# Token-major last products in the second block, and the first mixer's chunks in another order

## The reference

```python
# first block, layer 0: the first mixer (pool_hgrn_mixer), for both streams
z = h @ w_in                                   # u | q | zf | zb | v | g
f = lb + (1 - lb) * sigmoid(zf);  k, logf = 1 - f, log(f)      # and the same for zb
o = hgrn_scan(silu(q), k, v, logf)             # forwards and backwards, decays exp(cumsum(logf))
y = concat([multiscale_pool(u), rmsnorm(o) * silu(g)]) @ w_out
# every layer of the first block: six modulation vectors per layer and stream
m = silu(c) @ ada_w[l] + ada_b[l]
# second block, for each layer i, ALPHA = sqrt(2)
x = layer_norm(ALPHA * x + 0.5 * swiglu(x), g0, b0)
x = layer_norm(ALPHA * x + mixer(x), g1, b1)   # layer 0: window attention + gated recurrence; layer 1: delta rule
x = layer_norm(ALPHA * x + 0.5 * swiglu(x), g2, b2)
x = x + sigmoid(x @ ple_wg + ple_bg) * (p @ ple_wp)
# swiglu(x) = (silu(x @ wg) * (x @ wu)) @ wd, hidden width 2816
```

## Time and profile before

| | |
|---|---|
| median of 3 runs | 2632.01 us (2630.17 to 2641.66) |
| profiled execution | 2630.2 us, span 2628.4 us |
| TensorE busy | 2366.0 us, 90% |
| VectorE, ScalarE, GpSimd busy | 1277.7, 894.1, 120.1 us |
| last chain, share of TensorE | 84% |
| mean granted TensorE clock | 0.945 of full |
| moved from HBM | 370.64 MB, 141 GB/s over the span |

### The profile page before, as it was taken

One profiled execution on the slowest core, in us unless ns is written; L12 is line 12 of the kernel. 1 busy time (PEld: TensorE's weight loads), 2 busy tenths in 40 slices (PEclk: granted clock), 3 DMA queues, 4 the chain that ended last, 5 costly groups with the idle time before them and its releaser, 6 DMA issues.

```text
span 2628.4 us, 39106 instructions
## 1 busy us (share of the span) xinstructions
PE 2366.0 (90%) x17300; PEld 2181.0 (83%) x17300; DVE 1277.7 (49%) x1457; ACT 894.1 (34%) x929; POOL 120.1 (5%) x68
## 2 busy tenths in 40 slices
PE   7988888998899788999799878998899898888997
PEld 5876755998899556999799868998799795878996
DVE  4246425554454243544544545544554586526444
ACT  4212313334333132333433334333333434124332
POOL 0037400000000000000000000000000020000000
PEclk9988998999999999999899989999899996999998
DMA  7246701554355121355355313543354350013451
GB/s 304 98 164 262 289 16 60 180 188 160 133 187 177 71 88 64 144 184 184 128 185 177 129 69 126 188 176 142 130 186 181 108 182 16 1 66 135 177 188 35
DMA packets 52481, 373.10 MB, mean 142 GB/s; under 512 B 5728, under 2 KB 6752, under 8 KB 7840
## 3 DMA queue, kind: packets, MB, share of 16 engines
q1 hardware_dynamic: 51584, 367.78, 38.4%
q0 software_dynamic: 800, 3.93, 0.4%
HBM read 370.64 MB, written 1.05 MB: 141 GB/s over the span
## 4 chain that ended last, share of the span: by engine, by line
PE 84%; DVE 10%; ACT 3%; POOL 1%; issue 1%; DMA 1%; SPq 0%; DVEq 0%; ACTq 0%; POOLq 0%
PE PS L342 10%; PE PS L343 10%; PE PS L344 10%; PE PS L189 7%; PE PS L357 6%; PE PS L356 6%; PE PS L355 6%; PE PS L298 4%; PE PS L645 2%; DVE ring_r L443 2%; PE PS L280 2%; PE PS L263 2%; PE PS L265 2%; PE PS L264 2%; PE PS L281 2%; PE PS L282 2%
## 5 line engine op out<-in xcount | busy, mean ns | idle before, releaser
L443 DVE TENSOR_TENSOR ring_r<-ring,AR_r 128x2048 fp32r<-128x2048 f32 x274 | 625.0, 2289 | 605.8 <-ACT AR_r L437 595.4
L437 ACT ACTIVATE AR_r<-ring 128x2048 fp32r<-128x2048 f32 x274 | 520.1, 1908 | 705.4 <-PE PS L357 306.2
L342 PE MATMUL PS<-AR_r 128*128 128x256 f32 x2240 | 635.3, 284 | 0.0
L343 PE MATMUL PS<-AR_r 128*128 128x256 f32 x2240 | 634.7, 283 | 0.0
L344 PE MATMUL PS<-AR_r,ring_r 128*128 128x256 f32 x2240 | 634.6, 283 | 0.0
L342 PEld LDWEIGHTS PS<-AR_r 128*128 128x128 f32 x2240 | 430.9, 192 | 0.0
L343 PEld LDWEIGHTS PS<-AR_r 128*128 128x128 f32 x2240 | 430.9, 192 | 0.0
L344 PEld LDWEIGHTS PS<-AR_r,ring_r 128*128 128x128 f32 x2240 | 430.9, 192 | 0.0
L355 PE MATMUL PS<-AR_r 128*128 128x256 f32 x1232 | 348.7, 283 | 0.0
L356 PE MATMUL PS<-AR_r 128*128 128x256 f32 x1232 | 348.7, 283 | 0.0
L357 PE MATMUL PS<-AR_r,ring_r 128*128 128x256 f32 x1232 | 348.6, 283 | 0.0
(11 more groups left out here) (346 smaller groups left out, 3290.8 us busy)
## 6 DMA issues: line engine op xcount, KB each, us to landing
ring<-stream SPq DMA_DIRECT2D x346, 1024.0 KB, 4.8
X<-xt SPq DMA_DIRECT2D x1, 2048.0 KB, 10.1
AR<-bias POOLq DMA_DIRECT2D x1, 1536.0 KB, 6.8
AR<-pt POOLq DMA_DIRECT2D x2, 512.0 KB, 3.8
out<-X SPq DMA_DIRECT2D x1, 1024.0 KB, 4.8
SM<-small SPq DMA_DIRECT2D x1, 545.0 KB, 4.1
AR<-invc SPq DMA_DIRECT2D x1, 512.0 KB, 15.3
X<-negl POOLq DMA_DIRECT2D x1, 512.0 KB, 4.0
```

The lines of the kernel that those rows point to most:

```text
L342: pe.matmul(o, w_hi, X_HI[:, k, :], start=(k == 0), stop=False)
L343: pe.matmul(o, w_hi, X_LO[:, k, :], start=False, stop=False)
L437: act.activation(W_HI[i % 3], ring[:, n % SLOTS, :], ACT.Identity).then_inc(split_hi, 1)
L443: dve.tensor_tensor(RING_R[:, n % SLOTS, :], ring[:, n % SLOTS, :], W_HI[i % 3], ALU.subtract).then_inc(split_lo, 1)
```

## The change

Two things change.

In the second block the last products of the six stages come out token-major: token on the partition, feature along the row. The activation is stationary, and 512 columns of weights move past it (`down_tokens`, `pe_out_tokens`). The residual, scaled by 2 ALPHA or ALPHA, is put into the same banks by 16 fp32 matmuls with a scaled identity (`pe_residual_into_tokens`). The LayerNorm then takes its statistics along the row on VectorE (BN_STATS, BN_AGGR), ScalarE makes one column of Ln and Exp, both engines scale half a row each, and TensorE transposes back. The first two chunks of the next stage are split ahead. In the last mixer the logits come behind the first chunks, and the decay rows behind the first convolution.

In the first mixer the chunks come in the order zf, zb, u, q, g, v. Gates, logarithms, running sums and keys (`forget`, `keys_and_sums`), the pooling on GpSimd and the key sum (`KSUM`) have their places between the chunks' splits. The diagonal comes right behind the last chunk, two groups of modulation rows follow instead of six, and the levels hold 18 groups instead of 14. Rows of a batch of up to 12 groups gather in one bank, each at its own offset of the strips `CS`, and are copied and turned together.

```diff
-        EARLY_GROUPS = range(ADA_FIRST, ADA_FIRST + 6)
+        ADA_BATCHES = [range(0, ADA_FIRST), range(ADA_FIRST, 12), range(12, ADA_GROUPS)]
+        EARLY_GROUPS = range(ADA_FIRST, ADA_FIRST + 2)
...
+            def down_tokens(d, i, last, r):
+                n = n0 + i
+                need_split(r, i)
+                for t in range(2):
+                    for h in range(2):
+                        o = PS[:, 2 * t + h, :]
+                        for f in range(2):
+                            w = slice(f * D + h * 512, f * D + (h + 1) * 512)
+                            w_hi, w_lo = W_HI[i % 3][:, w], RING_R[:, n % SLOTS, w]
+                            ts = slice(t * P, (t + 1) * P)
+                            pe.matmul(o, G_HI[:, d, f, ts], w_hi, start=False, stop=False, skip_group_check=True)
+                            pe.matmul(o, G_HI[:, d, f, ts], w_lo, start=False, stop=False, skip_group_check=True)
+                            ins = pe.matmul(o, G_LO[:, d, f, ts], w_hi, start=False, stop=(last and f == 1), skip_group_check=True)
+                        if last and (t, h) != (1, 1):
+                            ins.then_inc(S["tokens_done"], S.mark("tokens_done", (tag, t, h)))
...
+            for t in range(2):
+                act.wait_ge(S["token_stats"], S.at("token_stats", (tag, t)))
+                act.activation(RSTD[:, t:t + 1], MEANVAR[:, t, 1:2], ACT.Ln, bias=EPS[:, eps:eps + 1]).then_inc(order.sem, order.step())
+                act.wait_ge(order.sem, order.n)
+                act.activation(RSTD[:, t:t + 1], RSTD[:, t:t + 1], ACT.Exp, scale=-0.5).then_inc(S["rinv"], S.mark("rinv", (tag, t)))
...
             pool.wait_ge(S["counts_loaded"], S.at("counts_loaded"))
-            pool.wait_ge(S["taken_vector"], S.at("taken_vector", 11))
+            pool.wait_ge(S["taken_vector"], S.at("taken_vector", 5))
...
                 dve_split_chunk(dve, "mix3_in", i + 3)
+                if i == 0:
+                    decay_rows()
```

More of the change, by code:

```diff
@@ L226, in pe_ada_rows @@
+        batch_of = lambda g: next(b for b, gs in enumerate(ADA_BATCHES) if g in gs)
+        ends_batch = lambda g: any(g == gs[-1] for gs in ADA_BATCHES)
         def pe_ada_rows(pe, g):
+            b = batch_of(g)
+            row = 2 * (g - ADA_BATCHES[b][0])
+            if row == 0:
+                pe.matmul(PS[:, b, 0:2], ZERO[:, :], ZERO[:, 0:2], start=True, stop=False, skip_group_check=True)
             for c in range(2):
[L229 removed]
@@ L364, in pe_ffn @@
                 pe.wait_ge(S["residual"], S.at("residual", (earlier, GROUPS - 1)))
-            for b in range(4):
+            for b in range(4) if not token_major else ():
                 pe.matmul(PS[:, b, 0:2], ZERO[:, :], ZERO[:, 0:2], start=True, stop=False, skip_group_check=True)
@@ new lines, in keys_and_sums @@
+            def keys_and_sums(d):
+                dve.wait_ge(S["log_forget"], S.at("log_forget", d))
+                dve.tensor_scalar(K2[:, d, :], K2[:, d, :], -1.0, 1.0, ALU.mult, ALU.add).then_inc(order.sem, order.step())
+                b = B2[:, d, ::-1] if d else B2[:, d, :]
+                for h in range(HEADS):
+                    bh = b[:, h * T2:(h + 1) * T2]
+                    ins = dve.tensor_tensor_scan(bh, RI[:, :], bh, 0.0, ALU.mult, ALU.add)
+                    if h < 3:
+                        ins.then_inc(order.sem, order.step())
+                ins.then_inc(S["log_sums"], S.mark("log_sums", d))
@@ new lines, in pe_out_tokens @@
+        def pe_out_tokens(pe, tag, x):
+            for i in range(4):
+                n = START[tag] + i
+                need_chunk(pe, n)
+                for t in range(2):
+                    for k in range(DT):
+                        ins = pe.matmul(PS[:, 2 * t + i // 2, (i % 2) * 256:(i % 2 + 1) * 256], x[:, k, t * P:(t + 1) * P],
+                                        ring[:, n % SLOTS, k * 256:(k + 1) * 256], start=False, stop=(i % 2 == 1 and k == DT - 1), skip_group_check=True)
+                    if t == 0 and i % 2:
+                        ins.then_inc(S["tokens_done"], S.mark("tokens_done", (tag, t, i // 2)))
+                ins.then_inc(multiplied, 1)
@@ new lines, in pe_layernorm @@
+        def pe_layernorm(pe, tag):
+            for first in (0, 4):
+                for t in range(2):
+                    pe.wait_ge(S["normed"], S.at("normed", (tag, t if first == 0 else 1)))
+                    pe.wait_ge(S["token_high"], S.at("token_high", (tag, t if first == 0 else 1)))
+                    for k in range(first, first + 4):
+                        ins = pe.transpose(turned_at(k)[:, t * P:(t + 1) * P], TOK[:, t, k * P:(k + 1) * P], IDENT)
+                        if t and k % 2:
+                            ins.then_inc(S["turned_back"], S.mark("turned_back", (tag, k // 2)))
```

405 lines of the change are left out of this document (220 added, 185 removed).

## The result

The changed kernel takes 2533.3 us (median of 4 runs, 2532.5 to 2534.4), the kernel before 2635.0 in the same comparison (2630.2 to 2641.7). The ratio is 0.9613, 95% interval 0.9589 to 0.9637; 2520 was forecast, in a range of 2502 to 2544. The profiled execution took 2532.5 us around a span of 2530.8 (before: 2630.2 and 2628.4), so the traces explain 97.6 us of span, and the prediction's sum was 111.2.

What follows compares the result with a forecast made beforehand. TensorE was taken to hold most of the chain, so time is won where it waits or multiplies less. Seven terms sum to 111.2 us off 2630.2, giving 2519, or 2520 against the median; range 2502 to 2544.

Steps and rivals of the forecast that it cites:

- Transfers in the levels: First mixer's levels: 88 us against 98.4, 10.4 us won, allowing 2 for late transfers; the transfers called the doubtful part.
- rival 1: First mixer's levels: transfers bind there, priced at 8 us by the scaled row, giving 2528; chance 0.12.
- The scaled 384: Old level loop's queue rate, 296 GB/s at share 0.77, scaled to a full share; it would give 8 us of waiting.
- The start of the levels: First mixer: the first level product starts at 181.7 instead of 220.1, 38.4 us won.
- rival 3: First mixer: GpSimd and VectorE slow each other more under the projection; 17 us lost, 2537; chance 0.05.
- The down products: Second block: 5.44 us a chunk instead of 5.76, residual +2.8; net 3 us won over four stages.
- rival 4: Down products: wide matmuls with gated activation as weights don't pipeline; slower than before, 2645 and up; chance 0.02.
- The LayerNorm behind a mixer: Second block, two stages: first chunks done at 17.0 against 28.3 us, at full clock; 22.6 us won.
- E+5.3: Behind a mixer: first weight product starts 5.3 us after E, the end of TensorE's last product.
- The LayerNorm behind a feed-forward: Second block, three stages: first product 7.6 us after the last, first chunks taking 12.6; 24.3 us won.
- Rival 2: LayerNorm chain: longer than built, half clock in all six stages; 2.5 us a stage, 15 in all, 2535; chance 0.14.
- ffn4 to the last mixer: Fourth feed-forward stage into last mixer: logits behind first chunks, a 1.9 us stall at chunk 4; 8.9 us won.

Runs made afterwards that it cites:

- half_rows: Changed kernel with only half of each transfer loaded for the 40 chunks of modulation rows behind the projection, matmuls as many as before; 2532.1 us.
- best: Changed kernel with LayerNorm statistics ahead of scaling, last modulation-row copy behind the exponentials, 20 identity transposes in one wait behind a feed-forward stage; 2516.5 us.
- warm_tr: Changed kernel with 16 and 18 identity transposes on TensorE in its LayerNorm waits behind each of the four feed-forward stages; 2519.6 us.
- logits_first: Changed kernel with the last mixer's logits back ahead of its first two chunks and the decay rows ahead of the first convolution; 2532.1 us.
- before_warm: Kernel before with 88 identity transposes on TensorE in its 12 us wait ahead of the first level product; 2629.6 us, ratio 0.9960.
- rows_late: Changed kernel with ScalarE's last modulation-row copy behind the exponentials and first key decay, and VectorE taking the modulation behind the scaled queries; 2532.1 us.

## Why the prediction was right, and where it was short

The forecast was right, and not because errors cancelled: all seven terms came out smaller than I took them, by 0.5 to 5.3 us.

**Transfers in the levels (rival 1).** The doubtful part held. The queue moves nearly what the first row promised (427 GB/s for 12 us) for 50 us on end; two windows of the changed kernel:

```profile
225.00:245.00 20.00, 20.00 (x242) 16.26 (x241) 20.00 (x20) 5.74 (x3) 16.52 (x7) 1.00 1.01 422
245.00:275.00 30.00, 28.00 (x353) 21.04 (x352) 21.87 (x27) 5.74 (x3) 16.88 (x7) 1.00 1.01 419
```

The scaled 384 was no limit. Nor was the 358 that the Trainium skill (DMA: Bandwidth & Descriptors, Where 436 GB/s comes from) gives for reads from HBM, as half of what two cores share: this kernel, on one core, gets 419 to 422. I allowed 2 us for late transfers; half_rows measures 2.6. TensorE's own work is as costed: 14 products spaced 3.71, 18 groups (1.87, 1.80 in pairs) and one turn make 86.0 where I had 86.2. The term is 2.4 short because I left out that VectorE's products hold TensorE for 1.4 us in steps 3 and 4, and the transfers cost 0.6 over the allowance; 0.4 are spread.

**The start of the levels** is 3.3 short. 1.6 of it is the projection, which starts later (65.03 for 63.40). The four first groups are now turned together behind ScalarE's copy; in the chain the last chunk of rows takes 1.98 there, half clock, and the copy 0.61 before the turn. I had costed the batched turn in the levels only. The other 1.6 is one link: I took 2.4 for VectorE's two products and they take 3.9, as they did before (2.74 and 1.15). Reorder and cover (rival 3) were right: the projection takes 110.09 as before, the diagonal follows the last chunk at once, and pooling ends at 151.4 and the key sum (L866) at 153.8, where I had 150 and 154:

```profile
150.08 1.29 POOL L967 TENSOR_TENSOR AR<-AR 128x512 f32<-128x512 f32 x1
...
151.48 2.29 DVE L866 TENSOR_TENSOR AR<-AR 128x2048 f32<-128x2048 f32 x1 [5.27 <-POOL AR L967]
```

**The down products** are spaced 5.47 a chunk (5.44 predicted), so rival 4 is out.

**The LayerNorm behind a mixer** was predicted at E+5.3 and full clock; it is 5.8 and full clock, the first chunks taking 11.7 (here the last product ends at 1537.56):

```profile
1543.39 0.36 PE L289 MATMUL PS<-AR_r 128*128 128x256 f32 x1 [1.59 <-DVE AR_r L494]
```

In `best`, though, one of the two began at half clock (13.9).

**The LayerNorm behind a feed-forward** is the step that was mis-sized, and 5.3 of the missing 13.8. "After a feed-forward I take 12.6": the first chunks take 13.6 to 14.2. BN_STATS is as assumed (0.65). The chain is 0.8 longer, mostly since twelve transposes run at half clock and four gain operations, not two, precede the first split. I had the mechanism, a clock that falls in the wait, but let the last transposes bring it back; warm_tr shows that this takes transposes before the fall. Rival 2 is thus a third true: the chain is 0.8 longer per stage, not 2.5.

**ffn4 to the last mixer**: 8.0 for 8.9, the stall at chunk 4 1.3 for 1.9. By logits_first at most 1.4 of it is the logits' move; the rest is the LayerNorm, which my sum did not separate.

**What the profile did not tell**: the medians differ by 101.7, the profiles by 97.6. The profiled execution of before was its fastest, and in the traces at hand the old levels are where its executions part.

## What to carry to other kernels

A wait that TensorE spends idle can be paid twice, in the wait and at half clock behind it, so an order that shortened it by 1.9 us of 8.4 won nearly twice that; where it can't be shortened, transposes of a constant hold the clock, if they stand ahead of the wait that ends last and fit in it. In a chain of small operations over two halves, do both halves' statistics before either's scaling. And compare stretches between landmarks, not totals, when executions differ by more than the edit.

## What the runs showed of the hardware that was not expected

- Transposes hold the clock as fp32 matmuls do: 1.00 in both fills, 0.50 without. The prediction expected it from one row; here it is shown by experiment.
- TensorE at 100% busy with small products (128x64, 32-row tiles) can be at half clock: the level products take 3.7 or up to 7.1 us, in steps that no wait precedes (before_warm: 7.00 us busy of 7.00 at 0.50), and not in the same steps in every execution.
- The clock can hide a gain of several us from one trace: in rows_late 6.1 us won were 0.4 at the next landmark, in `best` the same edit left 6.8.
- One queue kept 419 to 422 GB/s for 50 us on this core.
